# A streamed mixture-of-experts block on one core: loads of two turns made slot by slot, and token rows gathered in pairs and transposed by the gather itself

## The reference, cut to what matters

```python
h2 = rmsnorm(x, norm2_g)                      # 256 x 1024
logits = h2 @ w_router + b_router             # 32 experts
top_v, top_i = top_k(logits, 4); gates = softmax(top_v)
for e in range(32):                           # tokens t that chose e
    gu  = h2[t] @ w_gate_up[e] + b_gate_up[e] # 1024 -> 2 x 1024
    gate = min(gu[:, :1024], 7); up = clip(gu[:, 1024:], -7, 7)
    act = (up + 1) * (gate * sigmoid(1.702 * gate))
    out[t] += gates[t, e] * (act @ w_down[e] + b_down[e])
x = x + out;  return rmsnorm(x, final_g)
```

## Time and profile before

| | |
|---|---|
| device time, median of 3 runs | 1141.51 us (1140.75 to 1142.64) |
| the profiled execution | 1142.35 us, its span 1140.4 us, mean granted clock 0.998 |
| PE busy | 1108.2 us, 97% |
| VectorE, ScalarE, GpSimd busy | 221.8, 146.2, 30.3 us |
| DMA | 434.49 MB, mean 381 GB/s; queue q1 (SP's) 89.2% of 16 engines |
| chain that ended last | PE 75%, DMA 22%, ScalarE 2%, VectorE 1% |
| L1313, up tiles | 2048 records, 461.3 us busy |
| L1327, down tiles | 1024 records, 226.8 us busy |
| L1284, gather | 264 records, 63.9 us busy |
| L1291, transposes of rows | 260 records, 42.7 us busy |

### The profile page before, as it was taken

How to read it: one execution, slowest core, us unless ns; L and a number is a source line. 1 busy time by engine, 2 the same in 40 slices (tenths; PEclk the granted TensorE clock), 3 DMA queues, 4 the chain that set the end, 5 groups by cost and what they waited for, 6 DMA issues and landing times.

```text
span 1140.4 us, 12368 instructions
## 1 busy us (share of the span) xinstructions
PE 1108.2 (97%) x5162; PEld 451.6 (40%) x5163; DVE 221.8 (19%) x548; ACT 146.2 (13%) x306; POOL 30.3 (3%) x43
## 2 busy tenths in 40 slices
PE   7999999999999999999999999999999999999997
PEld 5858887433333333333333333333333333333332
DVE  1264213321111111111111111111111111111112
ACT  1053120210001100000000000100000000000001
POOL 1250000000000000000000000000000000000000
PEclk9999999999999999999999999999999999999999
DMA  9944366489999999999999999999999999999993
GB/s 361 412 142 179 113 252 223 153 353 409 429 434 428 437 425 438 425 438 426 438 426 438 426 437 428 436 429 434 430 433 431 432 432 431 433 429 434 430 423 132
DMA packets 26725, 434.49 MB, mean 381 GB/s; under 512 B 6416, under 2 KB 6672, under 8 KB 8912
## 3 DMA queue, kind: packets, MB, share of 16 engines
q1 hardware_dynamic: 22208, 430.32, 89.2%
q10 hardware_dynamic: 4496, 3.87, 1.1%
HBM read 433.14 MB, written 1.05 MB: 381 GB/s over the span
## 4 chain that ended last, share of the span: by engine, by line
PE 75%; DMA 22%; ACT 2%; DVE 1%; issue 0%; POOL 0%; DVEq 0%; SPq 0%; POOLq 0%
PE ps L1313 30%; DMA ring<-in_up 21%; PE ps L1327 14%; PE ps L1152 5%; PE ps L1284 4%; PE ps L1335 4%; PE ps L1166 2%; PE ps L1229 2%; PE ps L1041 2%; PE ps L1322 2%; PE ps L1291 1%; ACT work L615 1%; PE ps L1096 1%; PE ps L1060 1%; PE ps L1031 1%; PE ps L1297 1%
## 5 line engine op out<-in xcount | busy, mean ns | idle before, releaser
L1313 PE MATMUL ps<-ring,work 128*64 128x512 f32 x2048 | 461.3, 596 | 12.1 <-DMA ring<-in_up 11.5
L1313 PEld LDWEIGHTS ps<-ring,work 128*64 128x64 f32 x2048 | 141.0, 137 | 301.4 <-issue 281.1
L1327 PE MATMUL ps<-ring,work 128*64 128x512 f32 x1024 | 226.8, 595 | 0.6
L905 DVE TENSOR_SCALAR work<-ps 128x512 f32<-128x512 f32 x32 | 22.1, 692 | 673.6 <-PE ps L1313 673.6
L1327 PEld LDWEIGHTS ps<-ring,work 128*64 128x64 f32 x1024 | 70.7, 137 | 136.1 <-issue 127.9
L1335 PE MATMUL ps<-work 64*128 64x512 f32 x264 | 65.6, 615 | 0.8 <-ACT work L643 0.8
L1284 PE MATMUL ps<-work 128*64 128x512 f32 x264 | 63.9, 605 | 0.1
L1152 PE MATMUL ps<-work,ring 128*128 128x256 f32 x256 | 56.6, 379 | 0.0
L618 ACT ACTIVATE work<-ps 128x256 f32<-128x256 f32 x33 | 12.6, 383 | 336.5 <-PE ps L1297 336.5
L615 ACT ACTIVATE work<-ps 128x512 f32<-128x512 f32 x66 | 39.4, 597 | 104.8 <-PE ps L1284 80.1
L1152 PEld LDWEIGHTS ps<-work,ring 128*128 128x128 f32 x256 | 48.5, 190 | 6.6
(11 more groups left out here) (156 smaller groups left out, 540.2 us busy)
## 6 DMA issues: line engine op xcount, KB each, us to landing
ring<-in_up SPq DMA_DIRECT2D x60, 4096.0 KB, 38.1
ring<-in_down SPq DMA_DIRECT2D x29, 4096.0 KB, 35.4
ring<-in_front SPq DMA_DIRECT2D x22, 1024.0 KB, 17.7
ring<-in_up SPq DMA_DIRECT2D x16, 1024.0 KB, 5.4
ring<-in_down SPq DMA_DIRECT2D x12, 1024.0 KB, 9.6
ring<-in_front SPq DMA_DIRECT2D x2, 832.0 KB, 7.9
ring<-in_x SPq DMA_DIRECT2D x2, 512.0 KB, 4.0
ring<-in_x ACTq DMA_DIRECT2D x1, 1024.0 KB, 4.8
```

What stands on the lines that cost most here:

```text
L905: return dve.tensor_scalar(up_c, ps[:, UP, :], LIMIT, -LIMIT, ALU.min, ALU.max)
L1313: last = pe.matmul(ps[n * CAP:(n + 1) * CAP, bank, :], lhs(xT_e, k), w[bank - GATE][:, n * BANK:(n + 1) * BANK], start=k == 0, stop=k == K ...
L1327: last = pe.matmul(ps[n * CAP:(n + 1) * CAP, Y, :], lhs(actT, k), w[:, n * BANK:(n + 1) * BANK], start=k == 0, stop=k == KT - 1, skip_grou ...
```

## The change

1. The loads of turn 1 and turn 15 are issued slot by slot, each as soon as PE has freed its slot, and PE waits for them slot by slot (`fine`, `fine_load`). Turns 2 to 14 stay in groups. Turn 0 is as before.
2. The rows of two experts are gathered at once, and transposed: now a 128-column piece of `h2` is the weight (128 x 128), and `pick` moves, 128 columns for the two experts together. The result is already channels by tokens. There are 16 such products for a pair, eight channel pieces times two token tiles; four channel pieces fit a bank. The low four (`low`) are formed during the first expert of the pair, the high four during the second, one piece before the turn of the activation and three behind it. ScalarE copies each bank once (`take_xT`) into one of four homes, used in turns (`homes`).
3. The copy `take(x_e)`, the four transposes of rows, and the semaphores between them go. The gather writes the bank UP, so it waits for VectorE's clamp of that bank (`clamped2`). In the last two experts nothing more is gathered.
4. The first gather fills two banks. ScalarE copies the low half and VectorE the high half; VectorE's copy stands ahead of the chain that makes the routing weights. Both picks of the first pair are built before it. The transposing of the bias gates (`turn_gated(1)`) moves from before the first expert to behind its second tile.
5. Picks are built for a pair at the head of each even expert on VectorE, ahead of the clamps, no longer at the end of each expert.
6. The loop bodies on PE, ScalarE and VectorE hold four experts instead of two; PE's first and last four stand outside the loop.

```diff
-UNROLL = RING // PER_EXPERT
+PAIR = RING // PER_EXPERT
 SPAN = 4
-TURNS = E // UNROLL
+TURNS = E // PAIR
+UNROLL = 2 * PAIR
...
+        def homes(pair, high):
+            if pair % 2:
+                return xT[:, 2:4] if high else xT[:, 0:2]
+            return xT[:, 1:4:2] if high else xT[:, 0:3:2]
+
+        def fine(turn, at):
+            return turn in (0, 1, TURNS - 1)
...
+            def fine_load(i, at):
+                sp.wait_ge(freed, i * RING + (N_FRONT - RING + at + 1))
+                expert_load(i, at)
+
+            for at in range(RING):
+                fine_load(1, at)
-            with sp.Fori(1, TURNS - 1) as i:
+            with sp.Fori(2, TURNS - 1) as i:
                 for g in range(RING // SPAN):
                     group_load(i, g)
-            for g in range(RING // SPAN - 1):
-                group_load(TURNS - 1, g)
-            for at in range(RING - SPAN, RING):
-                sp.wait_ge(freed, (TURNS - 1) * RING + (N_FRONT - RING + at + 1))
-                expert_load(TURNS - 1, at)
+            for at in range(RING):
+                fine_load(TURNS - 1, at)
...
-            act.wait_ge(gathered, 1)
-            take(x_e).then_inc(xe_ready, 1)
-            act.wait_ge(xT_done, 1)
-            take(xT_e).then_inc(xT_ready, 1)
+            act.wait_ge(gathered_low, 1)
+            take_xT(0, 0, MIX).then_inc(xT_ready, 1)
...
-                    act.wait_ge(gathered, e + 2)
-                    take(x_e, Y).then_inc(xe_ready, 1)
-                    act.wait_ge(xT_done, e + 2)
-                    take(xT_e, UP).then_inc(xT_ready, 1)
+                    if not (isinstance(i, int) and e >= E - PAIR):
+                        act.wait_ge(gathered, e + 2)
+                        take_xT(u // PAIR + 1, u % PAIR).then_inc(xT_ready, 1)
...
-            build_picks(0, 0).then_inc(pick_ready, 1)
+            build_picks(0, 0)
+            build_picks(1, 1).then_inc(pick_ready, 1)
             normed(1, 1)
-            build_picks(1, 1).then_inc(pick_ready, 1)
...
+            dve.wait_ge(gathered, 1)
+            dve.tensor_copy(homes(0, 1).rearrange("p u k s -> p k u s"), ps[:, Y, :].rearrange("p (k u s) -> p k u s", k=4, u=2)).then_inc(xT_high, 1)
             dve.wait_ge(expo_ready, 1)
...
+                    if u % PAIR == 0:
+                        dve.wait_ge(gathered, e + 1)
+                        build_picks(0, e + PAIR)
+                        build_picks(1, e + PAIR + 1).then_inc(pick_ready, 1)
...
-                    build_picks(u % 2, e + 2).then_inc(pick_ready, 1)
...
+            def picked(bank, q, k, t, first, last):
+                return pe.matmul(ps[:, bank, q * 2 * CAP:(q + 1) * 2 * CAP], h2[:, t, k * P:(k + 1) * P], pick[:, t, :], start=first, stop=last,
+                                 skip_group_check=True)
+
+            def gather_first():
+                for t in range(TT):
+                    for k in range(KT):
+                        if k % 4 == 0:
+                            pe.wait_ge(h2_ready, 2 * t + k // 4 + 1)
+                        last = picked((MIX, Y)[k // 4], k % 4, k, t, t == 0 and k % 4 == 0, t == TT - 1)
+                        if t == TT - 1 and k == 3:
+                            last.then_inc(gathered_low, 1)
+                last.then_inc(gathered, 1)
+
+            def gather(k):
+                for t in range(TT):
+                    last = picked(UP, k % 4, k, t, t == 0, t == TT - 1)
+                return last
...
-            gather(0, first=True).then_inc(gathered, 1)
+            gather_first()
             open_sums(1, 1).then_inc(opened, 1)
-            pe.wait_ge(xe_ready, 1)
-            turn(x_e).then_inc(xT_done, 1)
-            pe.wait_ge(first_gates, 1)
-            turn_gated(1, Y).then_inc(first_ps, 1)
...
+                        if static and e == 0 and k == 4:
+                            pe.wait_ge(xT_high, 1)
+                        up_tile(homes(pair, k // 4)[:, b, k % 4, :], k, use(k), up_done).then_inc(freed, 1)
+                        if static and e == 0 and k == 1:
+                            pe.wait_ge(first_gates, 1)
+                            turn_gated(1).then_inc(first_ps, 1)
...
                     for n in range(2 * TT):
                         scatter(1 - b, n)
-                    pe.wait_ge(pick_ready, e + 2)
-                    gather(1 - b, Y).then_inc(gathered, 1)
+                    if following:
+                        if b == 0:
+                            pe.wait_ge(pick_ready, i * (UNROLL // PAIR) + (pair + 2))
+                        pe.wait_ge(clamped2, e + 1)
+                        gather(4 * b)
                     pe.wait_ge(gT_ready, e + 1)
                     pe.wait_ge(act_ready, e + 1)
                     turn(act_v).then_inc(actT_done, 1)
-                    pe.wait_ge(xe_ready, e + 2)
-                    turn(x_e, UP).then_inc(xT_done, 1)
+                    if following:
+                        for k in range(4 * b + 1, 4 * b + 4):
+                            last = gather(k)
+                        last.then_inc(gathered, 1)
                     pe.wait_ge(actT_ready, e + 1)
```

More of the change, by code:

```diff
@@ L217, in build @@
         h2 = held(0, TT, D)
-        x_e = held(2048, BANK)
-        xT_e = held(2560, BANK)
-        gate_c, up_c, sig, y_e = (held(3072 + n * BANK, BANK) for n in range(4))
+        xT = held(3072, 4, 4, CAP)
+        xT_over = held(3072, KT, CAP)
+        gate_c, up_c = (held(2048 + n * BANK, BANK) for n in range(2))
+        sig, y_e = (held(4096 + n * BANK, BANK) for n in range(2))
         actT, act_v = gate_c, up_c
-        pick = held(5120, 2, TT, CAP)
+        pick = held(5120, TT, 2 * CAP)
         gated = held(5376, 2, TT, P)
@@ L890, in build_picks @@
                 for t in range(TT):
-                    last = dve.tensor_scalar(pick[:, b, t, :], slots, places[:, t, bass.ds(je, 1)], None, ALU.is_equal)
+                    last = dve.tensor_scalar(pick[:, t, b * CAP:(b + 1) * CAP], slots, places[:, t, bass.ds(je, 1)], None, ALU.is_equal)
                 return last
@@ L1276, in _, with gather_over @@
             open_sums(1, 0)
-            def gather(b, bank=MIX, first=False):
+            def picked(bank, q, k, t, first, last):
+                return pe.matmul(ps[:, bank, q * 2 * CAP:(q + 1) * 2 * CAP], h2[:, t, k * P:(k + 1) * P], pick[:, t, :], start=first, stop=last,
+                                 skip_group_check=True)
+            def gather_first():
                 for t in range(TT):
-                    if first:
-                        pe.wait_ge(h2_ready, 2 * t + 2)
-                    for n in range(2):
-                        last = pe.matmul(ps[n * CAP:(n + 1) * CAP, bank, :], pick[:, b, t, :], h2[:, t, n * BANK:(n + 1) * BANK],
-                                         start=t == 0, stop=t == TT - 1)
+                    for k in range(KT):
[9 more added lines that the diff above has]
+                return last
+            def gather_over():
+                for k in range(KT):
+                    for t in range(TT):
+                        last = pe.matmul(ps[:, MIX, k * CAP:(k + 1) * CAP], h2[:, t, k * P:(k + 1) * P], pick[:, t, 0:CAP], start=t == 0, stop=t == TT - 1)
                 return last
@@ L1355, in experts @@
                     b = u % 2
+                    pair = u // PAIR
                     def use(j):
-                        at = u * PER_EXPERT + j
-                        if isinstance(i, int) and (i == 0 or at >= RING - SPAN):
-                            pe.wait_ge(loaded[at], 16 * (front_loads(at) + 1 + (i > 0)))
+                        at = u % PAIR * PER_EXPERT + j
+                        turn = i * (UNROLL // PAIR) + pair
+                        if static and fine(turn, at):
+                            pe.wait_ge(loaded[at], 16 * (front_loads(at) + sum(fine(n, at) for n in range(turn + 1))))
                         elif at % SPAN == 0:
-                            pe.wait_ge(grouped[at // SPAN], i * 16)
+                            pe.wait_ge(grouped[at // SPAN], i * (16 * UNROLL // PAIR) + 16 * (pair - 1))
                         return halves(at)
                     for k in range(KT):
-                        up_tile(b, k, use(k), up_done).then_inc(freed, 1)
+                        if static and e == 0 and k == 4:
[4 more added lines that the diff above has]
+                            turn_gated(1).then_inc(first_ps, 1)
                         if k == 5:
                             pe.wait_ge(gated_ready, e + 1)
+                            if static and e == 0:
+                                pe.wait_ge(y_ready, 1)
                             turn_gated(b).then_inc(gT_done, 1)
@@ L1372, in experts @@
                             up_biases(b)
+                    following = not (static and e >= E - PAIR)
                     pe.wait_ge(y_ready, e + 1)
```

53 lines of the change are left out of this document (26 added, 27 removed).

## The result

| | before | after |
|---|---|---|
| device time, median | 1141.28 us (1140.75 to 1142.64) | **1134.3 us** (1133.66 to 1135.41) |
| ratio, 95% interval | | 0.9936 (0.9924 to 0.9948) |
| the profiled execution, its span | 1142.35, 1140.4 | 1134.09, 1132.3 |
| PE busy | 1108.2 us, 97% | 1091.9 us, 96% |
| chain that ended last | PE 75%, DMA 22% | PE 65%, DMA 32% |

The change is faster by 7.0 us, 0.6%. The forecast of 1130 had the direction, and its range of 1126 to 1136 holds the result, but it promised 4 us more than came.

What follows compares the result with a forecast made beforehand. The bound was taken as one gapless weight stream plus PE's work after its last landings; 4.8 - 0.8 + 6.4 + 1.4 = 11.8 us off the profiled 1142.35 gave 1130.5, as median 1130 us, range 1126 to 1136.

Steps and rivals of the forecast that it cites:

- rival C: Last turn: the last loads land bunched, so 6.4 us of the gain is gone, 1136 us; chance 4%.
- Term 1: Start of the first expert: first tile at 232.1 instead of 231.65, first scatter at 248.2 instead of 247.2.
- Term 2: PE's pace: down starts 4.3 us after the scatters, so an expert takes 26.75 us instead of 27.67.
- Rival B: Gather: its weights cost openly, 3.5 us more before the first expert and 1.76 in each; 1139 us; chance 6%.
- Term 3: Turns 1 and 2: the stream becomes gapless earlier, third group of turn 2 landing at 328.1 before 332.7; gain 4.8 us.
- Term 4: Last turn: 20 slots now come singly at 2.47 us instead of 2.43, 0.8 us lost.
- Rival A: Single loads are slow, 3.07 us a slot, so 12.9 us are lost, 1154.5 us; chance 5%.
- Term 5: After the last up load: scatters start earlier, 6.4 us gained, and down follows them sooner, 1.4 us gained.
- L: The time when slot 19, the last up load of the last turn, lands; scatters were forecast 2.3 us later.
- The other two costs are nothing: SP's 24 single load issues instead of six, and PE's loop body of four experts, were taken to cost nothing.
- The 9.5 us after the last down product stay: Tail: the time from the last down product to the end was taken as unchanged, 9.5 us.
- Rival D: Last turn: PE waits at each slot and the clock falls to 1.2 GHz, about 1146 us; chance 3%.

Runs made afterwards that it cites:

- pair_only: The changed kernel with the loads of turns 1 to 15 as before (groups, only the last four slots single): 1143.73 us, ratio 1.0018 to the kernel before.
- fine_only: The kernel before with the loads of turns 1 and 15 made single, rows gathered as before: 1135.3 us, ratio 0.9944 to the kernel before.
- all_fine: The changed kernel with single loads in turns 2 to 14 as well: 1151.91 us, ratio 1.009 to the kernel before.
- early_open: The changed kernel with the last residual product ahead of the first gather and slot 23 of turn 0 loaded earlier: 1134.43 us, ratio 0.9938 to the kernel before.
- fine_first: The changed kernel with single loads in turn 1 and groups in turn 15 (last four slots single): 1140.55 us, ratio 0.9995 to the kernel before.

## Why the prediction was right, and why 4 us of it didn't come

**What bounds the kernel** was read rightly: a gapless stream from turn 2 on whose start is set in turn 1, and PE's work behind the last landing. pair_only shows it most sharply: 0.9 us less on PE in each of 30 experts, and the last big landing no earlier. That the result lies in the range is in part luck. The forecast's own range was 1128 to 1133.5, and only the widening for rival C, which didn't happen, takes in 1134.3.

**Term 1, the start.** First tile forecast at 232.1, measured 232.79; first scatter 248.2, measured 248.88. The gather was sized well (3.84 with its drain, 0.22 a product), but it began 0.4 later than forecast (228.16 for 227.75, behind the picks), and the first tile came 0.95 behind the start of the residual's product at 231.84.

**Term 2, the pace.** Forecast 26.75, measured 26.77. Rival B is out: the 128-column weights hide beside the products.

**Term 3, the gapless stream.** The mis-sized term is "Gain 4.6 to 6.4; I take 4.8". Slot 23 of turn 1, and the second and third group of turn 2:

```profile
L362 SPq DMA_DIRECT2D ring<-in_down x1: 327/327/327, 287.1 to 287.1; - x1
...
DMA to landing us min/median/max: 12.2/12.2/12.2
...
L393 SPq DMA_DIRECT2D ring<-in_up x1: 342/342/342, 302.7 to 302.7; - x1
...
DMA to landing us min/median/max: 16.4/16.4/16.4
...
L393 SPq DMA_DIRECT2D ring<-in_down x1: 333/333/333, 314.0 to 314.0; - x1
...
DMA to landing us min/median/max: 14.8/14.8/14.8
```

The third group landed at 328.8, 9.7 behind the second (319.1): it was not tight, and the stream had no gap there. Its 14.8 is that of the earlier trace rows by chance. The step "By the row of turn 1, 14.8 from issue to landing" took for fixed what depends on the loads ahead: the third group of turn 2 took 13.7 in fine_only, that of turn 1 13.0 in pair_only, both without a gap. The allowance for a gap (327.9 for 326.3) was thus 1.6 too much, but slot 23 landed at 299.3 for the forecast 297.2. Slot 0 came 0.7 later than forecast (240.7) and slot 1 0.6 late behind it. Slot 6, issued at 246.1, took 11.0 and landed 3.5 behind its forerunner, with one instruction fetch between 254 and 258, which cost 1.0; a fetch at 298.9 cost the first group of turn 2 another 0.3. Two errors nearly cancel, and the gain is 3.9, from 332.7.

**Term 4, the stream's speed.** Forecast 2.47 a slot, measured 2.48 to 2.49 (slot 18 at 1106.06, slot 19 at 1108.5), and 2.85 once, at slot 3 of turn 15 (landing at 1068.8), with a fetch at 1066.1: 0.3 and 0.4 us more over 20 slots. Rival A, 3.07 a slot, is out. The Trainium skill ("DMA: Bandwidth & Descriptors", Bandwidth) gives 341 GB/s for 1 MB, for DMAs issued from GpSimd. The queued 1 MB loads of all_fine moved 422 GB/s, so for a full queue the measurement decides against that row. The prediction's "The trace agrees for lone loads" is not shown: no load here was alone. Slot 23 of turn 0 took 4.6 us with its forerunner landing 1.8 us after its issue, and in the window of 341 GB/s in the earlier trace rows loads landed 2.4 to 2.9 us apart.

**Term 5, the end.** "They start at L + 2.3" held: landed 1108.5, scatters 1110.86. "3.8 after" held: 3.9. Landings came in even steps, so rival C is out. What failed is L itself, forecast 1105.7: 0.9 from term 3, 0.7 from term 4, 0.9 from the late load at 1019.6, 0.3 from the other 74 groups between (0.2 of it at one, landing at 377.6, with a fetch at 374.4). A faster stream in the last turn alone would have brought 0.3 more: in early_open, where PE alone stands behind the same landing, the last down starts 65.7 after it (1048.60 to 1114.27), here 66.0.

**The step behind most of the missing time** is "The other two costs are nothing", for "the PE loop body of four experts", and that fetches were priced nowhere. The loads that came late with a fetch lost 1.0 + 0.3 + 0.2 + 0.9 + 0.4 = 2.8 us up to the last up landing, where the other misses (slots 0 and 1, the slot price, the allowance for a gap) nearly cancel, and the tail lost 0.9. Not all of it is the loop body's: the kernel before has a fetch at 256.7 too. I asked of a fetch only whether PE would wait for its code, and with 2.4 us to spare it doesn't. The Trainium skill ("Runtime: NRT & Kernel Launch", Instruction fetch mechanics) has the same view: a fetch by the engine's own queue, mostly hidden, or a stall of that engine at a taken branch. The runs showed a third way: the fetch takes time on a DMA engine that the weights need. With it fell "The 9.5 us after the last down product stay": 1132.3 - 1121.86 = 10.4, by a fetch among the stores.

**Rival D** was wrong in its place and right in its kind. In the last turn the clock stayed at 1.00, but with a thinner PE each group wait further up is longer, 2.1 us for 1.3 in the kernel before. Two windows of the kernel after, up to the end of such a wait and behind it:

```profile
924.00:931.30 7.30, 5.20 (x26) 1.46 (x22) 0.00 (x0) 0.00 (x0) 0.00 (x0) 1.00 1.00 431
931.30:934.70 3.40, 3.34 (x10) 1.18 (x12) 0.00 (x0) 0.00 (x0) 0.00 (x0) 0.58 0.92 395
```

PE idles 2.1 us at full clock, and behind that the granted clock is 0.58 of 2.4 GHz, so mostly the lower level, 1.2 GHz. It fell behind five of the kernel's eight waits of 2.1 us and stayed at 1.00 behind the other three, and it never fell behind the waits of 1.3 us of the kernel before; what decides between equal waits is open. In the kernel after this hides under the stream; in fine_first it cost 1.7 us on the path.

The chain of the forecast ended at 1105.7 + 2.3 + 3.8 + 7.1 + 9.5 = 1128.4; the span is 1132.3. Of the 3.9 between them 2.9 stand at the scatters (2.8 of it the later L), 0.1 between scatters and down, 0.9 in the tail.

## What to carry to other kernels

In a kernel bound by a stream of weights, ask of every change when the stream becomes gapless and what stands behind its last landing; PE time saved between the two is worth nothing, and one that delays the first place freed can cost. Read the stream by the step from one landing to the next: the time from issue to landing has the loads ahead in it. Make loads fine only at the two ends of the stream, and coarse between. Count code as traffic: a longer loop body or tail is fetched by the DMA engines that carry the weights and the results, and what it delays is a load, not the engine that runs it.

## What the runs showed of the hardware

- Loads in a full queue: 432 GB/s with runs of 32 KB, 428 with 16 KB, 422 with 8 KB (1 MB loads). A run cost some 0.012 us beside 0.301 for each 8 KB, an estimate from the queue's share.
- 25 more instruction fetches of 16 KB cost 4.5 us in a stream-bound kernel, 0.18 us each on average. One could cost up to 1.4, when a load had to wait for it, and most cost nothing visible.
- SP's own issue stalls with many loads outstanding: with 9 to 12 of them, in turn 15 a single load took 2.1 us to issue in the median, 10.2 at the most, instead of 0.33. With 4 to 8 it took 0.33. It was harmless, since only further loads stood behind it.

```profile
L362 SPq DMA_DIRECT2D ring<-in_up x16: 328/2132/10214, 1013.3 to 1080.9; - x16
```

- Behind 2.1 us of idle PE the granted clock was 0.58, and 16 records took 5.35 us instead of 3.65, five times of eight in the kernel after; the other three times they took 3.65. In all_fine, where PE's idle time (27.5 of 640 us in the window above) comes in short waits for single slots, it stayed at 1.00.
